# Expert rows of a product-key retrieval kept as two tables, gathered in 4 KB rows, on one Trainium2 core

## The reference, cut to what matters

```
def block(args):
    xt, it, gt = args                    # 128 tokens, their 128 expert numbers, their gates
    u = expert_u[it]
    h = jax.nn.gelu(jnp.einsum('td,tkd->tk', xt, u), approximate=False)
    v = expert_v[it]
    return jnp.einsum('tk,tkd->td', gt * h, v)

y = lax.map(block, (xb, ib, gb))
return _rmsnorm(x + y, final_norm)
```

## Time and profile before

| | |
|---|---|
| median of three runs | 3771.78 us |
| the profiled execution's own time | 3772.01 us |
| its span, first to last instruction | 3770.2 us |
| busy: PE, DVE, POOL, ACT | 3089.4, 1844.8, 1135.2, 916.0 us |
| mean granted TensorE clock | 0.884 |
| expert stage, first gather to the end | 2387.0 to 3770.2 us |
| gathers: queue q0 | 536.90 MB |
| all HBM reads | 663.63 MB |

### The profile page before, as it was taken

The page is one execution under the profiler, slowest core; times in us unless marked ns, Lnnn a source line. Parts: engine busy times, 40 slices in busy tenths (PEclk is TensorE's granted clock), DMA queues, the critical chain, the costliest instruction groups (busy, mean ns, idle before and its releaser), DMA issues.

```text
span 3770.2 us, 37935 instructions
## 1 busy us (share of the span) xinstructions
PE 3089.4 (82%) x13628; PEld 2176.1 (58%) x13628; DVE 1844.8 (49%) x3736; ACT 916.0 (24%) x1539; POOL 1135.2 (30%) x744
## 2 busy tenths in 40 slices
PE   6987899998957998999559899877787687778776
PEld 4865799995834986778557677523333233323322
DVE  1054233303844632230861233477777777777765
ACT  2243333223353212332221433111111111111110
POOL 2300234342410000333420243333444344334432
PEclk8988899999976975999765999898999899999899
DMA  3200122222300000222010222599999999999998
GB/s 106 73 12 1 45 74 91 85 96 95 95 22 1 1 23 0 84 85 85 15 45 1 62 89 86 210 399 402 393 412 399 396 390 403 395 398 410 396 401 348
DMA packets 115311, 671.70 MB, mean 178 GB/s; under 512 B 16360, under 2 KB 17512, under 8 KB 49008
## 3 DMA queue, kind: packets, MB, share of 16 engines
q0 software_dynamic: 73728, 536.90, 34.8%
q1 hardware_dynamic: 31536, 114.83, 9.7%
q10 hardware_dynamic: 9920, 18.26, 1.4%
HBM read 663.63 MB, written 6.32 MB: 178 GB/s over the span
## 4 chain that ended last, share of the span: by engine, by line
PE 62%; DVE 14%; DMA 12%; issue 5%; ACT 5%; POOL 1%; DVEq 1%; ACTq 0%; PEldq 0%; POOLq 0%; PEld 0%
PE ps L871 13%; DMA arena<-in_experts,arena 12%; PE ps L387 11%; PE ps L388 11%; PE ps L389 11%; DVE arena L1824 1%; PE ps L713 1%; PE ps L804 1%; PE ps L806 1%; PE ps L650 1%; PE ps L723 1%; PE ps L756 1%; PE ps L754 1%; PE ps L558 1%; DVE h_all L1686 1%
## 5 line engine op out<-in xcount | busy, mean ns | idle before, releaser
L871 PE MATMUL ps<-arena 128*128 128x512 f32 x2048 | 981.9, 633 | 321.6 <-DVE arena L1829 320.1
L1848 POOL TENSOR_TENSOR ring_r<-ring,w_hi 128x1024 fp32r<-128x1024 f32 x215 | 520.1, 2420 | 1731.8 <-ACT w_hi L897 1545.7
L871 PEld LDWEIGHTS ps<-arena 128*128 128x128 f32 x2048 | 400.2, 202 | 896.8 <-issue 448.7
L1882 POOL DMA_INDIRECT arena<-in_experts,arena x512 | 553.5, 1081 | 801.0 <-PE ps L871 744.3
L1824 DVE SCALAR_TENSOR_TENSOR arena<-arena,ring 128x1024 f32<-128x1024 f32 x512 | 618.7, 1223 | 269.6 <-DMA arena<-in_experts,arena 240.6
L387 PE MATMUL ps<-n_hi,w_hi 128*128 128x264 f32 (+1 forms) x1744 | 587.4, 337 | 78.7 <-ACT slot_r L917 23.1
L389 PE MATMUL ps<-n_hi,ring_r 128*128 128x264 f32 (+1 forms) x1744 | 579.7, 332 | 0.0
L387 PEld LDWEIGHTS ps<-n_hi,w_hi 128*128 128x128 f32 x1744 | 333.8, 191 | 123.5 <-issue 31.8
L388 PE MATMUL ps<-slot_r,w_hi 128*128 128x512 f32 x896 | 358.1, 400 | 0.0
L389 PEld LDWEIGHTS ps<-n_hi,ring_r 128*128 128x128 f32 x1744 | 334.4, 192 | 33.4
L897 ACT ACTIVATE w_hi<-ring 128x1024 fp32r<-128x1024 f32 x171 | 181.1, 1059 | 661.9 <-PE ps L389 652.0
(11 more groups left out here) (322 smaller groups left out, 4386.1 us busy)
## 6 DMA issues: line engine op xcount, KB each, us to landing
ring<-in_weights SPq DMA_DIRECT2D x215, 512.0 KB, 3.5
arena<-in_experts,arena POOLq DMA_INDIRECT x512, 13.6
arena<-low_rest ACTq DMA_DIRECT2D x2, 2048.0 KB, 11.2
h_all<-in_xT ACTq DMA_DIRECT2D x1, 2112.0 KB, 16.7
h_rest<-h_all ACTq DMA_DIRECT2D x1, 2048.0 KB, 7.1
low_rest<-slot_r ACTq DMA_DIRECT2D x1, 2048.0 KB, 7.5
h_all<-h_rest ACTq DMA_DIRECT2D x1, 2048.0 KB, 10.2
out<-w_hi_f SPq DMA_DIRECT2D x4, 512.0 KB, 7.6
```

The lines of the kernel that those rows point to most:

```text
L871: last = mm(ps[:, yb + half, :], diag[:, j, :], uv[:, j, D + half * 512:D + half * 512 + 512], start=False, stop=False)
L1848: g_.tensor_tensor(ring_r[:, n % RING], ring[:, n % RING], w_hi[:, n % PAIR].bitcast(F32), ALU.subtract).then_inc(w_ready, 1)
L1882: g_.indirect_dma_start(uv[:, n % UV, :], None, experts, bass.IndirectOffsetOnAxis(ap=idxu[:, n // PAIRS, e:e + 1], axis=0)).then_inc(uv_i ...
```

## The change

The host no longer puts `expert_u` and `expert_v` side by side; they stay two tables with rows of 4 KB. Each step issues two indirect DMAs of 512 KB in place of one of 1 MB, with a semaphore per slot for each half. The gather of `u` waits for `dots` of the step eight before, that of `v` for `v_used` as before. DVE waits for `u_in` ahead of a dot product, and for `v_in` ahead of the diagonal, which is what PE's use of `v` hangs on. The bytes gathered, the eight slots, and all arithmetic are the same.

```diff
-        uv_in = [sem(f"uv_in{i}") for i in range(UV)]
+        u_in = [sem(f"u_in{i}") for i in range(UV)]
+        v_in = [sem(f"v_in{i}") for i in range(UV)]
...
                             for sl in (2 * g, 2 * g + 1):
-                                dve.wait_ge(uv_in[sl], (i + (first + 1)) * 16)
+                                dve.wait_ge(u_in[sl], (i + (first + 1)) * 16)
                                 last = v.scalar_tensor_tensor(uv[:, sl, 0:D], uv[:, sl, 0:D], 1.0, h2tok[t], ALU.mult, ALU.mult,
                                                               accum_out=hdot[:, sl:sl + 1])
                             last.then_inc(s["dots"], 1)
                             dve.wait_ge(s["gelu"], i * (UV // 2) + (UV // 2 * first + g + 1))
                             for sl in (2 * g, 2 * g + 1):
+                                dve.wait_ge(v_in[sl], (i + (first + 1)) * 16)
                                 v.tensor_scalar(diag[:, sl, :], ident, hgel[:, sl:sl + 1],
...
                 if n >= UV:
+                    pool.wait_ge(s["dots"], (n - UV) // 2 + 1)
+                e = n % PAIRS
+                row = bass.IndirectOffsetOnAxis(ap=idxu[:, n // PAIRS, e:e + 1], axis=0)
+                g_.indirect_dma_start(uv[:, n % UV, 0:D], None, experts_u, row).then_inc(u_in[n % UV], 16)
+                if n >= UV:
                     pool.wait_ge(s["v_used"], n - UV + 1)
-                e = n % PAIRS
-                g_.indirect_dma_start(uv[:, n % UV, :], None, experts,
-                                      bass.IndirectOffsetOnAxis(ap=idxu[:, n // PAIRS, e:e + 1], axis=0)
-                                      ).then_inc(uv_in[n % UV], 16)
+                g_.indirect_dma_start(uv[:, n % UV, D:2 * D], None, experts_v, row).then_inc(v_in[n % UV], 16)
...
-        "experts": np.concatenate([w["expert_u_2"][0], w["expert_v_2"][0]], 1),
+        "experts_u": w["expert_u_2"][0],
+        "experts_v": w["expert_v_2"][0],
```

More of the change, by code:

```diff
@@ L106, with build @@
 PARAM_W = _at
-def build(nc, xT, weights, params, consts, placing, toeplitz, sinks, keys, final_norm, experts, out):
+def build(nc, xT, weights, params, consts, placing, toeplitz, sinks, keys, final_norm, experts_u, experts_v, out):
     with ExitStack() as ctx:
```

## The result

The changed kernel takes 3886.61 us (median of four runs, 3875.91 to 3889.35); the kernel before took 3771.49 beside it (3764.91 to 3773.43). The ratio is 1.0303, with a 95% interval of 1.0279 to 1.0327. The profiled execution took 3883.95 us with a span of 3882.2, 112.0 us longer than before, at a granted clock of 0.876 (0.884 before). 1.9 us of that stand before the first gather, the rest lies in the expert stage.

The account below looks back on a forecast made before the run. The DMA engines bound the kernel at 2.61 us a step; POOL would take over at 2.48 + 0.46 = 2.94. 2417.8 + 1490.6 + 1.2 + 5.2 + 16.1 gave a span of 3930.9, so 3933 us, range 3830 to 4065.

Parts of the forecast that it names:

- POOL becomes the bound: Expert stage: POOL would need 2.94 us a step, above 2.65 for the DMA engines, and its idle time would go.
- forecast A: Whole kernel: POOL bound at 2.94 us a step, 3933 us; a pace of 2.85 to 3.10 gives 3887 to 4014; chance 0.66.
- Rival B: Expert stage: POOL bound but with the waits of today, 2.76 us a step, 3841 us; chance 0.12.
- 2.48 us a step for two gathers: POOL: two gathers a step at the old duration, 2 x (0.94 + 0.30) = 2.48 us.
- Rival F: POOL: gathers of 4 KB rows take less time, under about 0.75 us; pace 2.56 us, 3749 us, 0.6% faster; chance 0.05.
- 0.46 us a step for waits behind dot products: POOL: a dot product catches a gather's start 0.93 of the time, costing 0.515 us each; 0.48, rounded down to 0.46.
- The sum: Whole span: stage start 2417.8, steps 1490.6, second gather 1.2, landing 5.2, end 16.1; together 3930.9 us.
- Early release of `u` worth nothing: POOL's wait ahead of the gather of `u`: releasing its slot earlier costed at nothing; under 30 us if cover falls short.
- Rows at 2.65 us a step: DMA engines: 16 rows of 4 KB a step at 160 ns, 2.56 us, plus about 3%, 2.65 us.
- Rival E: DMA engines: 4 KB rows cost 209 ns like the weights' rows, 3.34 us a step, 4144 us; chance 0.06.
- DMA share to fall to 0.87: DMA engines in the profile after: share falls to about 0.87 and traffic to 355 GB/s.
- rival D: POOL: diagonals hold gathers as well, 0.26 us a step at worst, 3.20 us a step and 4065 us; chance 0.04.

Follow-up runs that it names:

- the pair of the third set: The changed kernel, 3893.51 us, and beside it the same kernel with the gather of `u` waiting for `v_used` in place of `dots`, 3894.39 us.

## Why the prediction was right, point by point

- **POOL becomes the bound**: shown. Its chain ends the stage, its waiting for slots is gone, and taking away what stretches its gathers gives 131 us back, where the loss on that chip was 124.
- **The figure**: 3933 forecast, 3886.61 measured. The pace, 2.84 us, lies a hair under the 2.85 at which forecast A's own band began, and above B's 2.76; the mechanism is A's, and one term of its sum was too large.
- **2.48 us a step for two gathers**: right, medians of 938 and 947 ns and 0.30 us between. Rival F needed gathers under 0.75 us: none was shorter than 0.93, even at 128 bytes a row.
- **0.46 us a step for waits behind dot products**: right in kind, too large. The gathers' means give 1.087 + 1.138 - 2 x 0.937 = 0.35, of which 0.32 behind dot products and 0.03 beside the selection, for which the forecast had no term. The mean gather was 1.11 us, where 1.15 to 1.2 was the sign given. The step that was off is "it catches a start 0.93 of the time, with 0.575 us still to run": there were 412 catches for 512 dot products, 0.80, at 0.396 us each and not 0.515. I took the mean over all phases, and the phases settle in part: 190 gathers start 1.02 to 1.20 us into a dot product, where next to nothing is left to wait for, and even phases would put 0.18 / 1.24 x 512 = 74 there. My reading of it is that a held gather starts over at the end of the dot product, so that the next start falls 1.24 us later, about when a second dot product right behind has ended too, as at 3021.88. Rival B, which had them settle fully at 2.76, lies as far off on the other side.
- **The sum**: forecast 3930.9 of span. Put right: +1.5 for the stage's later start (the gathers begin 1.9 us later, before any of them could matter), -50.5 for the pace (1440.1 in place of 1490.6), -1.2 as the last gather of `v` is off the chain, +1.4 for the landing (6.63, not 5.2) makes 3882.1, against 3882.2 measured.
- **Early release of `u` worth nothing**: shown, 0.9 us, by the pair of the third set.
- **Waits for `v_in` cost nothing**: right, DVE waited 1.2 us in all for landings of `v` in the stage.
- **Rows at 2.65 us a step**: 174 ns a row would be 2.79 us; that is no cost of the rows, for with POOL relieved the same rows went by in 2.60. Rival E, with 3.34, is out.
- **Landing to fall to about 5 us**: its median fell to 6.2.
- **DMA share to fall to 0.87**: wrong. The traffic fell (369 GB/s, forecast 355), the share didn't. I had read the share as "how full the engines are"; it counts the time from a packet's start to its end, and that stretched from 160 ns for half an 8 KB row to 174. In the run with the most traffic of this shape it reads 1.02. Only the GB/s told that the engines had room.
- **Diagonals hold gathers for next to nothing** (rival D out): 12 starts, 0.13 us. With one operand in PSUM, in the third set, 103 gathers started inside one; none took over 1.03 us, and they lost 1.5 us together. The Trainium skill, SBUF - State Buffer, "Who interferes with whom", has `tensor_scalar` among the operations that can enter a mode that shuts GpSimd out; these 128 x 128 ones in float32 didn't keep gathers out for their whole length. Its rule that a DVE instruction with two SBUF inputs contends with a GpSimd instruction that reads SBUF agrees with the runs: with one input in PSUM the mean gather fell from 1140 to 947 ns.

What the forecast did not have at all is the chip on which the same kernel takes 3991.

## What to carry to other kernels

Count what an engine pays per instruction before splitting transfers: here each indirect gather costs POOL 0.94 + 0.30 us for 128 rows, whether of 128 bytes, 4 KB or 8 KB, and what is held up by neighbours only shows once the slack is used. Keep one operand of long DVE instructions in PSUM where POOL issues gathers beside them: it was worth 131 us here with two gathers a step and 12 to 17 us with one. Only with one gather a step did a run copy every block's activations; what the copies would cost with two is not shown. Read GB/s beside the DMA share, and time an edit only against its base on the same chip.

## What the hardware showed beyond the expected

- **The same program differs by chip, and only in one of its forms.** The changed kernel took 3886.61, 3991.42 and 3893.51 us (the first result, the second set and the third), the kernel before 3771.49, 3767.65 and 3769.88 beside it. With early release taken back it was 4038.94 and 3894.39, with one operand in PSUM 3974.32 and 3762.11. What differs in the traces are late signals: waits on a semaphore that the own engine or a neighbour had raised end late on DVE, ACT, PE and POOL, on DVE up to 8.1 us late for a signal of its own. All six kernels with two gathers a step that ran in the first two sets had them; the two with one gather a step that were traced there had none, and the kernel before kept its time on both chips. Loading of code is not the reason in the stretch shown: the trace has no packet of instructions between 3141 and 3208 us. Why is open: neither fewer starts inside dot products nor a short pause removed them, and a POOL that issues far less often was not tried with two gathers. Whether it is the chip or its state at the time can't be told either, since no two sets shared a chip.
- **A gather's time on POOL doesn't depend on the width of its rows**: its median was 937 ns with rows of 8 KB and 938 with 4 KB, and 944 and 945 with 8 KB and 128 bytes side by side in one run.
- A gather of two rows per partition in one DMA, which might halve POOL's work, was not tried.
